# Expert weights in 1 MB loads with 8 KB per partition, and column groups of a mixture-of-experts layer worked on in twos

## The reference

```python
def swiglu(h, w_gu, w_down):
    g, u = jnp.split(h @ w_gu, 2, axis=-1)
    return (jax.nn.silu(g) * u) @ w_down

def moe_swiglu(h, w_router, w_gu, w_down):
    logits = (h @ w_router).astype(jnp.float32)
    top_vals, top_idx = lax.top_k(logits, TOP_K)
    top_w = jax.nn.softmax(top_vals, axis=-1)
    combine = jnp.sum(jax.nn.one_hot(top_idx, N_EXPERTS, dtype=jnp.float32) * top_w[..., None], axis=-2)
    ...
    for e in range(N_EXPERTS):
        out = out + combine[..., e:e + 1] * swiglu(h, w_gu[e], w_down[e])
    return out
```

## Time and profile before

| | us |
| --- | --- |
| three runs, median | 1515.46 (1513.43 to 1515.9) |
| profiled execution | 1516.27, its span 1514.5 |
| TensorE busy in the span | 1463.6 |
| VectorE, ScalarE busy | 988.8, 746.2 |
| mean granted TensorE clock | 0.996 of full speed |

### The profile page before, as it was taken

The page is one execution under the profiler, slowest core; times in us unless marked ns, Lnnn a source line. Parts: engine busy times, 40 slices in busy tenths (PEclk is TensorE's granted clock), DMA queues, the critical chain, the costliest instruction groups (busy, mean ns, idle before and its releaser), DMA issues.

```text
span 1514.5 us, 19554 instructions
## 1 busy us (share of the span) xinstructions
PE 1463.6 (97%) x6964; PEld 978.7 (65%) x6964; DVE 988.8 (65%) x1258; ACT 746.2 (49%) x977; POOL 13.8 (1%) x18
## 2 busy tenths in 40 slices
...
GB/s 363 320 272 287 250 392 308 295 287 305 68 228 167 98 101 262 249 308 329 410 409 409 401 409 408 372 411 400 409 409 409 409 409 399 409 409 408 392 409 266
DMA packets 156947, 501.90 MB, mean 331 GB/s; under 512 B 18483, under 2 KB 21196, under 8 KB 156840
## 3 DMA queue, kind: packets, MB, share of 16 engines
...
q0 software_dynamic: 1280, 4.01, 0.8%
...
## 4 chain that ended last, share of the span: by engine, by line
PE 83%; DMA 6%; DVE 4%; SPq 3%; ACT 2%; issue 1%; DVEq 0%; ACTq 0%
PE acc L2600 18%; PE acc L2608 17%; PE acc L2601 17%; PE acc L3097 14%; SPq L821 3%; DMA raw<-in_moe_w_down 2%; DVE w_lo L1517 1%; PE xb L2986 1%; PE acc L2749 1%; PE xb L3027 1%; DMA raw<-in_moe_w_gu 1%; DMA raw_more<-in_moe_w_gu 1%; DMA mod<-in_moe_w_down 1%; PE xb L2648 1%; PE acc L3221 1%
## 5 line engine op out<-in xcount | busy, mean ns | idle before, releaser
L1517 DVE TENSOR_TENSOR w_lo<-raw,w_hi 128x1024 fp32r<-128x1024 f32 x353 | 425.6, 1223 | 107.2 <-ACT w_hi L976 97.4
L976 ACT ACTIVATE w_hi<-raw 128x1024 fp32r<-128x1024 f32 x353 | 370.1, 1059 | 200.2 <-PE acc L2608 142.8
L2600 PE MATMUL acc<-w_hi,g_hi 128*128 128x512 f32 x448 | 179.1, 400 | 2.6 <-issue 2.6
L2601 PE MATMUL acc<-w_hi,g_lo 128*128 128x512 f32 x448 | 174.9, 390 | 0.0
L2600 PE MATMUL acc<-w_hi,a_hi 128*128 128x512 f32 x384 | 153.5, 400 | 0.8
L2601 PE MATMUL acc<-w_hi,a_lo 128*128 128x512 f32 x384 | 149.9, 390 | 0.0
L2608 PE MATMUL acc<-w_lo,g_hi 128*128 128x512 f32 x448 | 138.8, 391 | 1.7 <-DVE w_lo L1517 0.9
L3097 PE MATMUL acc<-raw,g_s 128*64 128x512 f32 x552 | 128.2, 597 | 0.0
L2608 PE MATMUL acc<-w_lo,a_hi 128*128 128x512 f32 x384 | 118.4, 390 | 0.0
L2600 PEld LDWEIGHTS acc<-w_hi,g_hi 128*128 128x128 f32 x448 | 84.1, 188 | 34.6 <-issue 15.2
L1517 DVE TENSOR_TENSOR w_lo<-mod,w_hi 128x1024 fp32r<-128x1024 f32 x68 | 82.3, 1222 | 27.0 <-ACT w_hi L976 24.3
...
## 6 DMA issues: line engine op xcount, KB each, us to landing
raw<-in_moe_w_gu SPq DMA_DIRECT2D x263, 512.0 KB, 12.5
raw<-in_moe_w_down SPq DMA_DIRECT2D x135, 512.0 KB, 15.1
raw<-in_ada_w SPq DMA_DIRECT2D x96, 512.0 KB, 5.9
mod<-in_moe_w_gu SPq DMA_DIRECT2D x90, 512.0 KB, 12.8
raw<-in_ffn_w_gu SPq DMA_DIRECT2D x56, 512.0 KB, 5.9
raw_more<-in_moe_w_gu SPq DMA_DIRECT2D x44, 512.0 KB, 12.2
mod<-in_moe_w_down SPq DMA_DIRECT2D x42, 512.0 KB, 15.2
raw<-in_ssm_w_in SPq DMA_DIRECT2D x40, 512.0 KB, 4.7
```

Of the source, the lines that this page charges most:

```text
L976: act.activation(w_hi[:, w % SPLIT, :], raw_tile(no), ACT.Copy).then_inc(hi_ready, 1)
L1517: dve.tensor_tensor(w_lo[:, w % SPLIT, :], raw_tile(no), r32(w_hi[:, w % SPLIT, :]), ALU.subtract).then_inc(raw_used, 1)
L2600: pe.matmul(o, l_hi[:, k, rows_], hi[:, col:col + HALF], start=new, stop=False)
L2601: pe.matmul(o, l_lo[:, k, rows_], hi[:, col:col + HALF], start=False, stop=False)
```

## The change

Five things change, all in the experts' section.

1. *Loads of two tiles.* MOE_LOADS holds pairs of tiles, each loaded by one DMA of 1 MB into two neighbouring homes. For two tiles of neighbouring column groups with the same k a partition's 8 KB is one run in memory: 2048 columns of one row of w_gu. For two w_down tiles the rows are dealt out anew: partition p takes rows 2p and 2p + 1 of a block of 256, again 8 KB in one run, and tile 2m holds the even rows, tile 2m + 1 the odd ones. Group 4, which stands alone, is loaded as two k tiles in one DMA with 4 KB runs. The homes raw_row and raw_rest, which are no neighbours, form a pair that is still loaded with two DMAs of 512 KB. A home pair is free when the later of its two tiles is used.
2. *Groups in twos.* The column groups run as (0, 2), (1, 3), (4), (5, 6); in a two, the tiles alternate: group 0 k 0, group 2 k 0, group 0 k 1 and so on, each group in an accumulator of its own (GROUP_HALF). The gates and products of a two stand together in the queues, two tiles after its end (GROUPS_DUE).
3. *Transposes.* Since the w_down tiles hold every other row, the transposes of the hidden values read every other column (`block_of`).
4. *Units.* Turns 0 and 1 are interleaved in units of 16, 16, 8 and 16 tiles, then 14 and 14 (large) or 8, 8, 6 and 6 (small), in place of 8 and 7, and turn 0 runs one unit ahead, not two. Transposes and gathers have new places (HIDDEN_AT, SMALL_SLOT_AT, GATHERS_AT).
5. *First loads.* The tiles of turn 0 that are loaded before the routing is known have a table of their own (FIRST_LOADS), 16 DMAs in place of 30.

```diff
-LARGE_AHEAD = 2
+LARGE_AHEAD = 1
...
+    GROUP_TWOS = ((0, 2), (1, 3), (4,), (5, 6))
+    GROUP_OF = [(js[n % len(js)], n // len(js)) for js in GROUP_TWOS for n in range(len(js) * KD)]
+    GROUP_OF += [(FJ, k) for k in range(FK)]
...
+    GROUP_HALF = (0, 0, 1, 1, 0, 1, 0)
+    GROUP_USE = (0, 1, 0, 1, 2, 2, 3)
+    GROUPS_DUE = {GROUP_END[js[0]] + 2: js for js in GROUP_TWOS}
+    HIDDEN_AT = (35, 37, 39, 59, 61, 63, 65)
...
-        steps = [KD] * FJ + [FK // 4] * 4
+        steps = [2 * KD, 2 * KD, KD, 2 * KD] + ([KD, KD, KD - 2, KD - 2] if p % 2 else [FK // 2, FK // 2])
...
+    FIRST_LOADS = ((14, "row_b"), (0, "more0", "more1"), (16, "once0", "once1"), (18, "once2", "once3"), (2, 4, 5), (4, 6, 7), (28, "mod0", "mod1"),
+                   (26, "once4", "once5"), (20, "once6", "once7"), (6, 8, 9), (8, 10, 11), (10, 0, 1), (12, 2, 3),
+                   (22, "mod2", "mod3"), (24, "mod4", "mod5"), (15, "rest8"))
...
+    homes_of_two = [(n, n + 1) for n in range(0, RAW + RAW_EXTRA, 2)]
+    for m, (p, n) in enumerate(MOE_SEQ):
+        if n % 2 == 0 and (p or n >= FIRST_TILES):
+            homes = min(homes_of_two, key=lambda two: max(held[two[0]], held[two[1]]))
+            if homes[0] == RAW:
+                for q in range(2):
+                    moe_load([(p, n + q)], [homes[q]])
+            else:
+                moe_load([(p, n), (p, n + 1)], list(homes))
...
-    SMALL_SLOT_AT = (35, 51, 59, 61)
+    SMALL_SLOT_AT = (36, 58, 60, 62)
+    GATHERS_AT = {0: (68, 72, 76), 1: (64, 68, 72)}
...
-            return q, self.used[q] + (0 if j == FJ else j // 2) + rep(self.e, moe_uses[q])
+            q = 2 if j == FJ else GROUP_HALF[j]
+            return q, self.used[q] + (0 if j == FJ else GROUP_USE[j]) + rep(self.e, moe_uses[q])
...
+    def block_of(m):
+
+        return slice(m // 2 * 2 * P + m % 2, (m // 2 + 1) * 2 * P, 2)
...
-        k = s - FJ * KD
-        return w_down[k * P:(k + 1) * P, :]
+        k, half = divmod(s - FJ * KD, 2)
+        return w_down[2 * k * P:2 * (k + 1) * P, :].rearrange("(p h) n -> p h n", h=2)[:, half, :]
...
+                home_used(before)
+                w_gu, w_down = A["moe_w_gu"][0, experts_[p]], A["moe_w_down"][0, experts_[p]]
+                if len(tiles) == 1:
+                    dst, src = raw_tile(nos[0]), mixture_source(w_gu, w_down, n)
+                elif n < FJ * KD:
+                    gi, k = GROUP_OF[n]
+                    if GROUP_OF[n + 1][0] == gi:
+                        dst = two_tiles(homes[0])
+                        src = w_gu[k * P:(k + 2) * P, MIX_COLS[gi]:MIX_COLS[gi] + TW].rearrange("(h p) n -> p h n", h=2)
+                    else:
+                        dst = two_tiles(homes[0]).rearrange("p h n -> p (h n)")
+                        src = w_gu[k * P:(k + 1) * P, MIX_COLS[gi]:MIX_COLS[gi] + 2 * TW]
+                else:
+                    k = n - FJ * KD
+                    dst = two_tiles(homes[0]).rearrange("p h n -> p (h n)")
+                    src = w_down[k * P:(k + 2) * P, :].rearrange("(p h) n -> p (h n)", h=2)
+                sp.dma_start(dst, src).then_inc(raw_ready[homes[0]], 16)
...
+                    for gi in GROUPS_DUE.get(s, ()) if B.mixture else ():
+                        mix_products(B, gi)
...
-                                mm = pe.transpose(b[:, m * P:(m + 1) * P], hidden[:, m * P:(m + 1) * P], ident)
+                                mm = pe.transpose(b[:, m * P:(m + 1) * P], hidden[:, block_of(m)] if B.mixture else hidden[:, m * P:(m + 1) * P], ident)
```

More of the change, by code:

```diff
@@ L445, in build, with keep_in @@
[L445 to L453 removed]
+    raw_home, raw_sem, raw_turn, turns, held = {}, {}, {}, {}, {}
+    def keep_in(nos, homes):
+        before = max((held[home] for home in homes if home in held), default=None)
+        turns[homes[0]] = turns.get(homes[0], 0) + 1
+        for no, home in zip(nos, homes):
+            raw_home[no], raw_sem[no], raw_turn[no] = home, homes[0], turns[homes[0]]
+            held[home] = no
+        return before
```

157 lines of the change are left out of this document (74 added, 83 removed).

## The result

| | before | changed |
| --- | --- | --- |
| median of the runs, us | 1515.68 (1513.43 to 1516.59, 4 runs) | 1526.71 (1525.40 to 1528.01, 4 runs) |
| span of the profiled execution, us | 1514.5 | 1523.6 |
| ratio | | 1.0074, 95% interval 1.0061 to 1.0087 |

The account below looks back on a forecast made before the run. Large turns were taken as bound by TensorE, ends of small turns by loads. By turn, 2.2 - 0.8 + 0.8 - 3.7 + 0.8 - 3.6 = -4.3 us gave 1511.2 us, range 1504.5 to 1519.5.

Parts of the forecast that it names:

- (2): Column groups in twos, large turns: waits on accumulators at groups' ends cost 2.2 us per large turn (bounds 0 and 5).
- the way down: Down projection's start in large turns: waits 1.2 us for group 5's accumulator, plus 0.2 for a weight load, 1.4 us.
- Group 4's start: In large turns, after group 1's end: wait of 0.6 us plus 0.2, 0.8 us.
- Rival C: Large turns: TensorE becomes the bound, each us of wait costs three times; at 5 us a turn 1519.6 us; chance 0.11.
- (1): Expert loads: 8 KB packets raise the rate to 420 GB/s, mean saving 0.031 us a tile (bounds 0 and 0.05).
- B: Expert loads: no gain from 8 KB, pieces move as 4 KB ones, rate stays 409 GB/s; 1519.5 us; chance 0.12.
- D: Expert loads: smaller gain, 0.014 us a tile by the skill's rule, 414 GB/s; 1515.2 us; chance 0.12.
- A: Loads' gain comes through whole because the accumulators' waits are hidden; 1504.0 us; chance 0.15.
- upper bound of 0.05 us a tile: Expert loads: largest saving from 8 KB pieces, described as a straight line through the 2 KB and 4 KB rates.
- (3): Homes released in pairs, at the loads' restart after the homes fill: 0, bounds -0.9 and +0.9 us.
- (4): First loads and longer units in turns 0 and 1: stock of landed tiles swings more; 0, bounds -1 and +3 us.
- three signs that the prediction is wrong: Profile after: rate stays at 409, large turns over 128 us, or turns 0 and 1 show waits for loads.

Follow-up runs that it names:

- e1: Changed kernel with VectorE reading the small turn's output right after turns 3 and 5, and after one tile in turn 1: 1515.43 us, ratio to before 1.0008.
- e3: Changed kernel with each pair of tiles loaded by two 512 KB DMAs with 4 KB pieces, same homes and releases: 1530.91 us.
- e9: e3 with each DMA waiting only for its own home's last tile, not for both homes of the pair: 1529.10 us.
- e2: e1 with each group's silu and products one tile after its own end, not two after the end of the two: 1518.28 us.
- e5: e1 with turn 1's silu and products of a two of groups two tiles later in the queues: 1514.00 us, ratio to before 1.0000.
- e6: e5 with group 5's products after tile 56's w_lo and group 6's after tile 57's: 1510.94 us, ratio to before 0.9976.

## Why the prediction was wrong

**The step that failed is (2), and in it the list of places.** The sum said -4.3 us, and +11 came. Of this gap of 15 us the large turns hold 11.5 (3.7, 5.8 and 5.8 in place of 2.2, 0.8 and 0.8), turns 0 and 1 hold 2.6 and small 3 holds 1.4. I looked for waits on accumulators where a group *ends* inside a turn, and priced these. The first opening of the second accumulator in a turn I did not look at. It moved from tile 8 to tile 1, and what it waits for is the last reader of the turn before. I had even followed that rule for the ends ("a group's pair is wanted again one tile after its end, not eight") without asking who else had been covered by the eight tiles. The reader was to be seen in the timeline of the kernel before:

```profile
1070.26 1.41 DVE L2026 TENSOR_TENSOR y_s<-acc,mod 64x512 f32<-64x512 f32 x2
```

It ends 7.5 us after the small turn's last tile began at 1064.20 and 5.1 us after the large turn's first at 1066.62. Against tile 1, 1.4 us after that first, this is a stop of over 3 us; against tile 8 it is nothing. The move of that reader alone (e1) gave back 10 of the 11 us.

**The prices inside (2) were right where I had a row.** For the way down I had taken from the earlier trace rows that the products are done 3.94 us after the last tile of the group starts, and a wait of 1.2 us. The changed kernel, turn 4:

```profile
1157.76 0.39 PE L2651 MATMUL acc<-w_hi,g_hi 128*128 128x512 f32 x1
...
1160.26 1.88 DVE L2134 TENSOR_TENSOR gate_l<-gate_l,acc 128x512 f32<-128x512 f32 x3
...
1161.68 0.47 PE L2651 MATMUL acc<-w_hi,e_hi 128*128 128x512 f32 x1 [1.04 <-DVE gate_l L2134]
```

1161.68 - 1157.76 = 3.92, and the start-to-start delay is 1.20 us with its weight load, where my 1.2 had the load's 0.2 on top. Group 4's start cost 0.28, not 0.8. So the groups' ends made 1.5 us a large turn, where I had 2.2. The missed place made 1.45 in turn 2, and 3.1 with 1.7 of low clock around it in turns 4 and 6.

**Rival C had the mechanism and the wrong place.** It said that TensorE becomes the bound in large turns, that each us counts once in each of three, and that it decides from 3.6 us a turn on, counted from a turn of 123.96 us. The turns took 3.6, 7.1 and 7.1 more than that. I gave it 0.11 because I looked for its cause at the groups' ends, where 5 us was indeed too much.

**(1) held.** 417 to 421 GB/s against the 420 worked out from the rows; B (409, nothing gained from 8 KB) is out, D's 414 is passed, and A is out, in which no wait of TensorE would count. Its upper bound of 0.05 us a tile was not what I called it: a straight line through 388 and 409 GB/s gives 451 at 8 KB, 0.12 us a tile. Nothing hung on it. The Trainium skill's rule ("DMA: Bandwidth & Descriptors", "Why small descriptors are slow") makes 8 KB an estimated 1.1% faster than 4 KB. Measured is 417 / 409, 2.0%, to 421 / 409, 2.9%. The small turns came near to what I had summed, 0.6 - 4.4 - 3.3 = -7.1 against -8.1: -0.8 forecast and +0.6 measured in small 3, -3.7 and -4.4 in small 5, -3.6 and -3.3 in small 7. Some of small 5's gain is not the pieces': while TensorE stood still in turn 4, the loads ran on and filled the homes, and e3, without the pieces, has a small 5 of 91.8.

**(3) was probably mis-sized.** I took 0 at the restart with bounds of 0.9. Small 3 came out 1.4 us longer than forecast, and e9's profile has a small 3 that is 1.6 us shorter without the release in pairs; the medians do not confirm it.

**(4) was put at 0, with a bound of +3; it was 2.6.** The reason I gave was a swing of the stock of tiles. The real one was ScalarE's queue, two tiles ahead instead of three behind a small unit twice as long (e2, e5).

**What I said would show it.** Of the three signs that the prediction is wrong one came: large turns of over 128 us (turns 4 and 6, 131). The rate did not stay at 409. Turns 0 and 1 do show waits, but for w_lo, not for loads as the sign had it, and it would have missed them. The dips of the rate before small 5 and 7 came as forecast: 254 GB/s from 1205 to 1207 us and 115 from 1427 to 1429.

Of the changed kernel's 11 us, e1 gives back 10, and with e5 and e6 it stands 0.24% below the kernel before. The remaining 0.4 us of turn 4 and 0.8 of turn 2 I have not assigned.
